# Another order of loads in the preparation, the attention output and the pooled unit of a two-block network

## What is computed

```python
mod = jnp.einsum('bd,de->be', jax.nn.silu(c), w_ada[l]) + b_ada[l]
shift, scale, gate = jnp.split(mod, 3, axis=-1)
h = rms_norm(x, norm_pre[l]) * (1.0 + scale[:, None, :]) + shift[:, None, :]
proj = jnp.einsum('bsd,de->bse', h, w_in[l])
...
mix = jnp.einsum('bse,ed->bsd', jnp.concatenate([ya, yb], axis=-1), w_out[l])
x = x + gate[:, None, :] * rms_norm(mix, norm_post[l])
...
# second block
h = modulate(x, norm1_g, shift, scale)
p = h @ w_in
diff = centred_window_mean(u, win) - u       # pooled unit, u from p, win in (2, 4, 8, 16)
y = jnp.einsum('blgc,gcd->blgd', diff, w_pool) * pool_scale
```

## Time and profile before

| | us |
|---|---|
| median of 3 runs | 1911.39 (1908.18 to 1918.78) |
| the profiled execution, its own time | 1913.7 |
| its span | 1911.8 |
| TensorE busy | 1720.0 (90%) |
| VectorE busy | 801.3 (42%) |
| ScalarE busy | 518.8 (27%) |
| POOL busy | 109.3 (6%) |
| waits of TensorE's products (L207) in all | 163.0 |

### The profile page before, as it was taken

How to read it: one execution, slowest core, us unless ns; L and a number is a source line. 1 busy time by engine, 2 the same in 40 slices (tenths; PEclk the granted TensorE clock), 3 DMA queues, 4 the chain that set the end, 5 groups by cost and what they waited for, 6 DMA issues and landing times.

```text
span 1911.8 us, 37762 instructions
## 1 busy us (share of the span) xinstructions
PE 1720.0 (90%) x16766; PEld 927.0 (48%) x16766; DVE 801.3 (42%) x1472; ACT 518.8 (27%) x983; POOL 109.3 (6%) x143
## 2 busy tenths in 40 slices
PE   4999999889998899989999999999969977777886
PEld 3444466444545655555666677544533323223332
DVE  3754153445626638345655555344441221212111
ACT  3620253221116612155453352121221110101010
POOL 0000010010000000020000000000010100000000
PEclk8999997999998999999998998999979999989898
DMA  9112284361111030042211210366479999999996
GB/s 390 73 51 81 104 299 172 143 257 76 44 44 45 1 127 1 1 175 78 86 58 59 75 48 31 113 249 243 177 278 389 419 424 418 423 418 422 415 407 208
DMA packets 51561, 359.43 MB, mean 188 GB/s; under 512 B 8393, under 2 KB 8641, under 8 KB 32961
## 3 DMA queue, kind: packets, MB, share of 16 engines
q1 hardware_dynamic: 38896, 311.51, 40.9%
q0 software_dynamic: 12496, 45.45, 7.2%
HBM read 337.99 MB, written 27.32 MB: 191 GB/s over the span
## 4 chain that ended last, share of the span: by engine, by line
PE 73%; DMA 17%; ACT 4%; DVE 3%; issue 2%; POOL 0%; SPq 0%; ACTq 0%; POOLq 0%; DVEq 0%
PE psum L207 69%; DMA arena<-in_w 16%; PE psum L210 4%; ACT arena L204 3%; ACT L204 1%; DVE arena L154 1%; DVE arena L164 1%; DVE arena L160 1%; DMA arena<-in_norm_post 1%; DMA arena<-in_subln 0%; DVE arena L159 0%; DVE arena L180 0%; DMA mods<-arena 0%; DVE arena L172 0%; SPq L143 0%
## 5 line engine op out<-in xcount | busy, mean ns | idle before, releaser
L207 PE MATMUL psum<-arena 32*32 32x16 f32 (+11 forms) x16114 | 1637.5, 306 | 163.0 <-DMA arena<-in_w 84.9
L207 PEld LDWEIGHTS psum<-arena 32*32 32x32 f32 (+5 forms) x16114 | 853.6, 135 | 895.8 <-issue 773.8
L204 ACT ACTIVATE arena<-psum 128x512 f32<-128x512 f32 (+5 forms) x334 | 171.4, 513 | 893.6 <-PE psum L207 666.4
L154 DVE TENSOR_TENSOR arena<-arena,psum 128x512 f32<-128x512 f32 (+3 forms) x128 | 64.9, 507 | 413.1 <-PE psum L207 225.0
L154 DVE TENSOR_TENSOR arena<-arena 128x512 f32<-128x512 f32 (+10 forms) x315 | 191.6, 608 | 50.4 <-ACT arena L204 14.8
L204 ACT ACTIVATE arena<-psum,arena 128x128 f32<-128x128 f32 (+3 forms) x221 | 111.7, 505 | 290.5 <-PE psum L210 157.0
L204 ACT ACTIVATE arena<-arena 128x512 f32<-128x512 f32 (+10 forms) x254 | 138.8, 546 | 172.3 <-DVE arena L154 38.4
L210 PE MATMUL psum<-arena 128*128 128x128 f32 x652 | 105.3, 294 | 18.4 <-DMA arena<-fd,arena 8.6
L210 PEld LDWEIGHTS psum<-arena 128*128 128x128 f32 x652 | 75.7, 148 | 77.7 <-issue 52.3
L154 DVE TENSOR_TENSOR arena<-psum,arena 128x128 f32<-128x128 f32 (+3 forms) x116 | 47.4, 409 | 152.2 <-PE psum L207 129.1
L164 DVE SCALAR_TENSOR_TENSOR arena<-arena 128x512 f32<-128x512 f32 (+7 forms) x158 | 102.1, 646 | 14.1 <-ACT arena L204 8.1
(11 more groups left out here) (49 smaller groups left out, 176.9 us busy)
## 6 DMA issues: line engine op xcount, KB each, us to landing
arena<-in_w SPq DMA_DIRECT2D x127, 2048.0 KB, 29.0
arena<-in_w SPq DMA_DIRECT2D x48, 256.0 KB, 3.0
arena<-in_w SPq DMA_DIRECT2D x10, 1024.0 KB, 19.2
arena<-kd POOLq DMA_DIRECT2D x28, 256.0 KB, 4.4
gd<-arena SPq DMA_DIRECT2D x24, 256.0 KB, 3.4
arena<-gd SPq DMA_DIRECT2D x24, 256.0 KB, 5.4
arena<-in_w POOLq DMA_DIRECT2D x2, 2048.0 KB, 9.4
kd<-arena POOLq DMA_DIRECT2D x2, 1536.0 KB, 11.0
```

The costliest lines, as they stand in the source:

```text
L154: return self.ends(self.e.tensor_tensor(out, a, b, op))
L204: return self.ends(self.e.activation(out, a, func, **kw))
L207: return self.ends(self.e.matmul(out, lhs, rhs, start=start, stop=stop))
```

## The change

Loads are asked for in another order and some engine programs are reordered to match. In the preparation the tokens are loaded before the weights; TensorE transposes the tokens after row 0; positions and w_rg are asked for once row 2 is done; the end of HT is signalled in two halves (`ht 2`, `ht 3`), and the products of the first projection wait for each half. In attention POOL loads the gate row and norm_post before it stores block 10. In the output stage the turn of yb 3 moves between `mix(1, 0)` and `mix(1, 1)`, and POOL loads ropes. In the second block pool_w is asked for first, without a wait for the end of the output stage, and ropes and pool_w have semaphores of their own. `Y` is SP, `G` POOL, `T` TensorE, `A` ScalarE, `V` VectorE.

```diff
@@ pre_sync
             Y.dma(cst, T_["consts"], d_cst.up("cst"))
-            load(0)
-            load(1)
             Y.dma(X, x_in, d_x.up("x"))
-            load(2)
-            load(3)
+            for c in range(4):
+                load(c)
@@ pre_tensor
             modulation_row(0)
+            for i in range(4):
+                T.wait_ge(V["n1", i])
+                turn8("f1", i, ht1[i], ALL8)
             modulation_row(1)
             modulation_columns(0)
             modulation_row(2)
             modulation_columns(1)
-            for i in range(4):
-                T.wait_ge(V["n1", i])
-                turn8("f1", i, ht1[i], ALL8)
+            modulation_columns(2)
             modulation_row(3)
-            modulation_columns(2)
             modulation_columns(3)
@@ pre_scalar
             A.act(sg, par[:, 0:24], ACT.Sigmoid).then_inc("cs_sg")
-            row(0)
-            row(1)
             A.wait_ge(d_x["x"])
...
-            row(2)
+            row(0)
             for i in range(4):
                 turn8_act("f1", i, HT, i)
-            row(3)
+            row(1)
+            row(2)
             A.wait_ge(V["f1", 3, 1])
             for j in (2, 3):
+                if j == 3:
+                    row(3)
                 A.wait_ge(V["gmod", j])
...
-            A.then_inc("ht")
+                A.then_inc("ht", j)
@@ pre_vector
-            columns(0)
             V.wait_ge(A["sq1"])
...
-            columns(1)
             for i in range(4):
                 turn8_dve("f1", i, HT, i)
+            columns(0)
+            columns(1)
...
-            V.then_inc("ht")
+                V.then_inc("ht", j)
@@ proj1_gpsimd
+            G.wait_ge(T["w", 2])
             G.dma(posb, T_["positions"][0, :].partition_broadcast(128), d_pos.up("pos"))
             G.dma(wbd, T_["w_rg"], d_wbd.up("wbd"))
-            G.wait_ge(A["ht"])
+            G.wait_ge(A["ht", 3])
@@ proj1_tensor
-            T.wait_ge(A["ht"], V["ht"])
...
                 for k in range(8):
+                    if t == 0 and k % 4 == 0:
+                        T.wait_ge(A["ht", 2 + k // 4], V["ht", 2 + k // 4])
@@ lru_gpsimd
             for j in range(4, 16):
+                if j == 10:
+                    G.wait_ge(V["yan"], *mods_stored(5))
+                    G.dma(G1, mods1[2048:3072].partition_broadcast(128), d_g1.up("g1"))
+                    G.dma(np_, T_["norm_post"].partition_broadcast(128), d_g1.up("np"))
                 ada_gpsimd(j)
@@ out1_gpsimd
-            G.wait_ge(T["pv1", 31], V["yb", 3], V["yan"], A["yr", 3], *mods_stored(5))
-            G.dma(G1, mods1[2048:3072].partition_broadcast(128), d_g1.up("g1"))
-            G.dma(np_, T_["norm_post"].partition_broadcast(128), d_g1.up("np"))
+            G.wait_ge(T["pv1", 31], V["ybt", 3], A["yr", 3], V["ada", 13])
+            G.dma(TB, T_["ropes"], d_rope.up("rope"))
@@ out1_tensor
             for i in range(4):
-                if i == 1:
-                    att_gated_tensor(3)
                 for hf in range(2):
+                    if (i, hf) == (1, 1):
+                        att_gated_tensor(3)
@@ proj2_gpsimd
+            G.dma(PW, T_["pool_w_2"][0].rearrange("g c d -> c g d"), d_pw.up("pw"))
             G.wait_ge(*end1(), *mods_stored(17))
-            G.dma(TB, T_["ropes"], d_tb.up("rope"))
-            G.dma(PW, T_["pool_w_2"][0].rearrange("g c d -> c g d"), d_tb.up("pw"))
@@ proj2_tensor
-                T.wait_ge(V["pool", m], d_tb["sub"], *ps.take(ALL8, "pw", m))
+                T.wait_ge(V["pool", m], d_pw["pw"], *ps.take(ALL8, "pw", m))
@@ proj2_vector
-                V.wait_ge(d_tb["sub"])
+                V.wait_ge(d_rope["rope"])
...
-            V.wait_ge(*end1(), *mods_stored(17))
+            V.wait_ge(*end1())
...
                     V.ts(P["qn"], P["qn"], 0.125, None, ALU.mult)
+                    V.wait_ge(d_tb["sub"])
```

More of the change, by code:

```diff
@@ L419, in build @@
         d_fd = [dma("fd0"), dma("fd1")]
+        d_rope, d_pw = dma("rope"), dma("pw")
         d_wp = [dma("wp0"), dma("wp1")]
```

## The result

| | before | after |
|---|---|---|
| median of the 20 runs of each in the first comparison | 1922.02 | 1901.24 |
| ratio after/before there | | 0.9934, 95% interval 0.9913 to 0.9955 |
| the same in two more sets | | 0.9915 (0.9886 to 0.9943), 0.9918 (0.9886 to 0.9950) |
| mean over the sets (before: without the first set) | 1917.1 (85 runs) | 1903.1 (36 runs) |
| profiled execution, span | 1913.7, 1911.8 | 1910.7, 1908.9 |

The change is faster. The ratios give 0.7 to 0.85%; the means lie 14.0 us apart, with standard errors of 0.6 and 1.0 us, so 14.0 ± 1.2. Taken set by set, before and after side by side, the differences of the means are 12.8 ± 2.3, 16.0 ± 1.7 and 15.7 ± 2.5 us, together 15.1 ± 1.2. The two executions profiled first lie only 3.0 us apart, and that gap between 3 and 14 is half of what there is to explain here.

A forecast was written before the change was run, and what follows sets the result against it. TensorE was 73% of the chain, DMA 17%. Gains 5.0 + 6.4 + 5.2 = 16.6 us took 1913.7 to 1897.1; with the median 2.3 lower, forecast 1895 (1890 to 1899 at 0.66), range 1887 to 1905.

The forecast's parts named there:

- Preparation, forecast 5: Start of the kernel: VectorE starts the rotary angles at 38.0 instead of 42.94; gain 5 us, bounds 2.5 and 6.5.
- the overlap at the end of the stage: End of preparation: TensorE's 16 products, started when w6 lands near 38.2, end at 53.9, under VectorE's 55.4.
- The figure for a POOL-issued load: Moved positions load: the skill page's fit gives 2.6 us to land, the trace 8.2 us; the forecast used 8.2.
- Attention output, forecast 6.4: Output stage: TensorE's idle 5.04 us behind mix(0,1) goes, plus 1.4 us of clock; gain 6.4 us, bounds 5.0 and 6.5.
- The bank: Output stage: yb 3's transposes take mix(0,1)'s PSUM bank, so TensorE idles 5.04 us until VectorE has copied it.
- the slack of 3.6 us: Output stage, token tile 0: VectorE's chain ends at 357.7, TensorE comes for it at 361.3.
- the price of the clock: Attention output: clock 0.64 over 3.8 us behind TensorE's idle time, 1.4 us gained with the wait removed.
- Pooled unit, forecast 5.2: Pooled unit: TensorE's 3.49 us wait for VectorE goes, plus 1.7 us of clock; gain 5.2 us, bounds 3.5 and 5.3.
- (b): Last stage's 104 weight loads absorb the gain, time stays 1911; milder, part lost to clock or another wait, 1903; together 0.11.
- (a): Preparation gives nothing because w3 or positions land 5 us later than worked out; 1900 us; chance 0.12.
- (c): Preparation: POOL's queue is starved, positions land late behind the weights and the kernel is slower, 1915 at 58; chance 0.03.
- (d): Output stage: another wait holds yb 3's bank in both forms, so that part's gain falls away; 1901 us; chance 0.03.

The follow-up runs named there:

- e4: The changed kernel, unaltered, profiled a second time; ratio to the kernel before 0.9915.
- e12: The changed kernel, unaltered, profiled a third time; ratio to the kernel before 0.9918.
- e7: The changed kernel with positions and w_rg asked for at the start again, as before; mean 1907.4 us against 1903.1, ratio to the kernel before 0.9970.
- e8: The kernel before with only the turn of yb 3 moved behind the first product sum of tile 1; ratio to the kernel before 1.0019.
- e9: The kernel before with only the gate row and norm_post asked for in attention; ratio to the kernel before 0.9990.
- e2: The kernel before with the attention output's edits alone; ratio to the kernel before 0.9967, span of its profile 1964.9 us.

## Why the prediction was right or wrong

**Preparation, forecast 5.** The path was right: X seen at 10.11 (10.9 in the text), w0 at 15.12 (16.2), row 3 done at 34.15 (34.8 to 36.4), angles at 37.34 (37.3 to 38.9), release at 54.76 (55.4). The step that failed was the overlap at the end of the stage: "it is done at 53.9, under VectorE's 38.0 + 17.4 = 55.4" leaves TensorE idle for 1.5 us, and I let the clock be full behind that, as it was behind the 1.51 us of before. In the first profile w6 was there at 36.99 and the products took 14.00 us, so TensorE was done at 50.99 and idled 3.77 us, and the clock fell behind it: 5.6 us at the release, 3.9 behind the clock. I had charged such a fall only to the waits that were removed. The second and third profile (e4, e12), TensorE's release and the stretch behind it:

```profile
55.07 20.30 PE L207 MATMUL psum<-arena 128*128 128x512 f32 x43 [2.43 <-DVE arena L164]
55.00:60.30 5.30, 5.23 (x9) 2.37 (x10) 2.82 (x5) 2.24 (x3) 0.00 (x0) 0.69 0.01 3
```

```profile
54.58 20.87 PE L207 MATMUL psum<-arena 128*128 128x512 f32 x48 [0.60 <-DVE arena L164]
36.00:42.80 6.80, 5.56 (x7) 2.47 (x8) 5.32 (x10) 1.25 (x1) 1.58 (x3) 0.50 1.01 427
54.50:60.00 5.50, 5.42 (x13) 2.55 (x14) 2.83 (x5) 5.20 (x7) 0.00 (x0) 1.00 0.01 3
```

VectorE releases TensorE at the same time to within 0.5 us in all three. In the third the slow stretch lies at 36.0 to 42.8, in the 16 products, where VectorE's chain hides it, and 5.8 us are gained; in the first two one lies behind the release and costs 1.6 to 1.7 us, and 3.9 and 3.7 are left. So the term of 5 measured 4.5 on average, and among these three it is where the slow stretch falls that tells 3.7 from 5.8. The deferral of positions was priced by its bytes, 1.8 us; e7 measured 3.6 at w0 and 3.1 at the release.

**The figure for a POOL-issued load.** Positions took 8.87 us from issue to landing; the row of before (8.2) was the right guide. It decided a wait of VectorE of 0.38 us here, none in the second profile and 1.40 in the third. The 2.6 us by the fit of the Trainium skill (DMA: Bandwidth & Descriptors, section Anatomy of one DMA) are again not what the trace has under load.

**Attention output, forecast 6.4.** 6.6 in each of the three profiles of the changed kernel. The bank, the slack of 3.6 us (VectorE is through at 350.65, TensorE comes at 354.18) and the price of the clock held. What the forecast did not say is that the two edits are each enough (e8, e9).

**Pooled unit, forecast 5.2.** 6.8 to 7.2. pool_w was issued at 399.17, landed after 4.5 us, in time. Of the 1.9 us above the forecast 1.3 is the first part of pool 0: its 8 products took 7.12 us, and 8.44 in the first profile of before, which has more of the lower clock behind the wait for w26. That is chance, and not the change: the second profile of before has 7.12 us as well. The removed wait is no fixed number either; it is 3.49 us in the first profile of before and 5.16 in the second, where TensorE arrives earlier.

**The sum and the forecast time.** The local sum, 16.6 forecast, was 17.6 in the first profile (3.9 + 6.6 + 7.1), 17.1 in the second and 19.6 in the third, against the first profile of before; against the second each is 1.0 larger. So the places and the waits were right, and the forecast time failed behind them, in two steps. The larger one is the level: 1911.39, the median of three runs, was 5.7 us below the mean of 85 (1917.1), so that 1895 should have read 1900.5. The second is that gains reach the end unchanged: by the pooled means 14.0 ± 1.2 us do, 2.6 less than forecast, and by the sets 15.1 ± 1.2. Together the two are the 8.3 us by which the mean, 1903.1, lies above the 1894.8 of the sum. The medians of the three sets, 1901.24, 1902.48 and 1902.76, lie above the 1890 to 1899 that got 0.66 and inside the wide range. The shortfall against the local sum, 2 to 4 us, is some two standard errors; e8, whose interval shuts out its local gain, points the same way. Of those 14.0, mean span times mean clock shows 9.8 us (1817.2 to 1807.4) and time lost to the lower clock 4.2 us (98.1 to 93.9); the forecast had 13.5 us of waits and 3.1 of clock. (The split is rough: in the product a wait that falls into a slow stretch counts half.) The mild form of rival (b), "part of the gain lost to the clock", happened in each profile by another amount.

**The rivals.** (a) did not happen. (b) as absorption by the last stage is refuted: the 104 loads start at 1318.34 in the first profile after, 2.5 us earlier as TensorE was by then, and the gain keeps to within a few us from 1245 to the end. (c) is refuted by 8.87 us, (d) by e8 and e9.

**What stays open.** Whether the early entry costs the recurrence something on average. Two profiles of before lose 0 and 1.4 us between 803 and 1245, the other kernels 2.5 to 17.3. That may be chance, or a systematic loss of a few us, which would be the missing 2 to 4. Against it: the first profile of before, with which all are compared, has the highest clock of all there, 0.97, so nearly any other loses; and the profile of e9, which enters 14.0 us late, loses 8.0 us too. Two profiles of before are too few, and no run here varied the entry alone.

## What to carry to other kernels

Price a removed wait with the slow clock behind it, and then look for the idle time that the new order itself leaves on TensorE: it can cost its own slow stretch, as it did in two of three profiles here. In e7 small loads in front of the stream of weights cost it up to twice their bytes, so ask for them only when a chain is about to need them. A gain of under 1% has to be read locally, stage by stage over matched instructions, and the level of a kernel from many runs: one pair of profiles said 3 us where the means say 14.

## What was not expected of the hardware

TensorE's granted clock differs between executions of one program (profiled here on different chips), enough to move a stage of 55 us by 9 us and one of 450 us by 13 (after, first and third profile). In the attention of the first block it stood at the lower level with TensorE busy throughout, mostly in narrow products (64 and 128 columns) and transposes; the first profile of before, and the second:

```profile
300.40:327.50 27.10, 27.10 (x174) 18.41 (x174) 5.58 (x10) 9.69 (x18) 1.19 (x3) 0.50 0.26 97
```

```profile
297.80:304.40 6.60, 6.60 (x41) 4.20 (x40) 1.39 (x3) 3.60 (x8) 0.00 (x0) 0.50 0.17 69
304.60:324.00 19.40, 19.40 (x230) 13.79 (x230) 6.53 (x12) 8.27 (x15) 2.19 (x4) 1.00 0.60 218
```

Its beginning is not chance: in both it comes some 1 us after TensorE has resumed (at 299.24 and 296.41) from a wait of 1.9 us, and all the other profiles but e2's, which is left out here, show it within 1.5 us of the end of that same wait. Its length is chance: from 7 to 27 us. Half the difference in length, 10 us, accounts for the 9.3 us between the two profiles of before. Over the runs of the changed kernel the mean clock went from 0.942 at 1914.8 us to 0.956 at 1892.1 in the first 20: most of the spread of this kernel is that.
